# Prompt values in fp32, query copies and rope keys moved ahead, pages turned by sequence and fetched in halves, in a two-layer MLA and RG-LRU decoding step

## The reference, cut to what matters

```python
def mla_scores(q_lat, q_pe, ckv, kpe):
    s = jnp.einsum('bthc,blc->bhtl', q_lat, ckv, preferred_element_type=jnp.float32)
    s = s + jnp.einsum('bthr,blr->bhtl', q_pe, kpe, preferred_element_type=jnp.float32)
    return s * SM_SCALE
```

## Time and profile before

| | us |
|---|---|
| median of 3 runs | 1817.2 (1814.12 to 1818.85) |
| the profiled execution | 1814.61 |
| its span, first to last instruction | 1812.8 |
| last pair of the prompt attention, its 16 steps | 62.2 |
| decode attention, up to the first turn of probabilities | 64.0 |
| decode attention, from there to the last value product | 360.0 |

### The profile page before, as it was taken

The page is one execution under the profiler, slowest core; times in us unless marked ns, Lnnn a source line. Parts: engine busy times, 40 slices in busy tenths (PEclk is TensorE's granted clock), DMA queues, the critical chain, the costliest instruction groups (busy, mean ns, idle before and its releaser), DMA issues. The chain is left out here.

```text
span 1812.8 us, 26109 instructions
## 1 busy us (share of the span) xinstructions
PE 1433.7 (79%) x10731; PEld 1138.1 (63%) x10731; DVE 785.7 (43%) x1099; ACT 521.2 (29%) x741; POOL 152.1 (8%) x132
## 2 busy tenths in 40 slices
PE   4679998598988889717878878779969999750697
PEld 1279997377776777613444444447849999750485
DVE  0151010547373645626666656523236620349532
ACT  3321112134242433301111111223333232463332
POOL 0000000000000000020111111001220000025122
PEclk7769999699999989958889888889979999875799
DMA  9921110210010100092666655225321110100322
GB/s 328 341 59 36 46 35 25 60 30 1 23 29 23 29 23 0 0 357 46 238 242 236 244 233 233 117 89 167 120 69 47 46 46 12 47 0 0 131 96 78
DMA packets 98192, 180.39 MB, mean 100 GB/s; under 512 B 14245, under 2 KB 68395, under 8 KB 94026
## 3 DMA queue, kind: packets, MB, share of 16 engines
q1 hardware_dynamic: 88906, 95.50, 16.5%
q0 software_dynamic: 9216, 83.89, 11.7%
HBM read 162.10 MB, written 14.65 MB: 98 GB/s over the span
## 5 line engine op out<-in xcount | busy, mean ns | idle before, releaser
L80 PE MATMUL bank<-in_x_hi,in_w_hi 128*128 128x272 f32 x992 | 289.2, 291 | 19.2 <-DVE in_x_lo L413 19.2
L81 PE MATMUL bank<-in_x_lo,in_w_hi 128*128 128x272 f32 x992 | 289.1, 291 | 0.0
L82 PE MATMUL bank<-in_x_hi,in_w_lo 128*128 128x272 f32 x992 | 288.7, 291 | 0.0
L80 PEld LDWEIGHTS bank<-in_x_hi,in_w_hi 128*128 128x128 f32 x992 | 189.3, 191 | 19.4 <-issue 19.3
L82 PEld LDWEIGHTS bank<-in_x_hi,in_w_lo 128*128 128x128 f32 x992 | 189.0, 190 | 0.0
L81 PEld LDWEIGHTS bank<-in_x_lo,in_w_hi 128*128 128x128 f32 x992 | 188.9, 190 | 0.0
L1201 PE MATMUL bank<-u_T,q_rows 32*64 32x512 f32 x2560 | 156.2, 640 | 33.2 <-DMA q_rows<-qpe_blocks 33.2
L1096 DVE STREAM_TRANSPOSE u_T<-ckv_pages 128x1024 f32<-128x1024 f32 x128 | 147.4, 1209 | 69.1 <-DMA ckv_pages<-in_cache_ckv,page_parts 68.7
L403 DVE TENSOR_TENSOR in_w_lo<-in_w_raw,in_w_hi 128x1024 fp32r<-128x1024 f32 x31 | 38.0, 1225 | 239.4 <-ACT in_w_hi L355 239.3
L1201 PEld LDWEIGHTS bank<-u_T,q_rows 32*64 32x64 f32 x2560 | 55.8, 144 | 124.1 <-issue 87.0
L80 PE MATMUL bank<-out_w_hi,out_g_hi 128*128 128x512 f32 (+1 forms) x288 | 115.0, 399 | 13.0 <-DVE out_w_lo L1428 13.0
(11 more groups left out here) (259 smaller groups left out, 2534.8 us busy)
## 6 DMA issues: line engine op xcount, KB each, us to landing
u_T<-in_w_ada SPq DMA_DIRECT2D x12, 2048.0 KB, 14.5
in_w_raw<-in_r_w_in SPq DMA_DIRECT2D x16, 512.0 KB, 3.8
in_w_raw<-in_a_w_in SPq DMA_DIRECT2D x15, 512.0 KB, 4.0
x_tiles<-in_x_prompt SPq DMA_DIRECT2D x8, 512.0 KB, 9.6
g_mid<-u_T SPq DMA_DIRECT2D x4, 1024.0 KB, 4.0
out_w_raw<-in_a_w_o SPq DMA_DIRECT2D x8, 512.0 KB, 7.0
u_T<-g_mid SPq DMA_DIRECT2D x8, 512.0 KB, 5.9
out_x_in<-in_x_prompt SPq DMA_DIRECT2D x8, 512.0 KB
```

The costliest lines, as they stand in the source:

```text
L80: pe.matmul(out, w_hi, x_hi, start=start, stop=False)
L81: pe.matmul(out, w_hi, x_lo, start=False, stop=False)
L82: return pe.matmul(out, w_lo, x_hi, start=False, stop=stop)
```

## The change

- `values` of the prompt attention is one fp32 product for each key block instead of three fp32r ones. `v_all` and `p_T` are plain fp32 copies. The subtractions for `v_lo` and `pt_lo` are gone, and with them the waits for them; `turn` and `values` wait for ACT's copy (`pt_sb`).
- `q_rows` is allocated earlier. SP copies the queries of the first two sequence pairs inside `prompt_attention`, once the last head pair's queries are kept, and before the last spill. The part ends when they have landed.
- POOL fetches the rope keys of steps 0 and 1 there too, once three spills are done.
- A step's first chunk is now the rope keys, and the four latent chunks follow. DVE's order in step x is: last latent chunk of x, rope keys of x + 1, `maximum(x)`, three latent chunks of x + 1 for sequence 0, the same for sequence 1, `accumulate(x - 1)`. The rope keys of step 0 are turned before the new tokens' scores. `ckv_in` and `kt_set` are counted by sequence.
- The latents are fetched in halves, 8 KB for each partition (8 of its 16 rows), two gathers each. The first half of x + 3 waits for the second quad of `values(x)`, the second half for the fourth. The rope keys of x + 2 are fetched when those of x are turned. POOL's order is rope keys of x + 2, then latents of x + 3. DVE makes the indices of the halves (`halves`) in two operations.

```diff
-    v_hi, v_lo = sb("v_hi", [P, 8, 2 * P], F32R), sb("v_lo", [P, 8, 2 * P], F32R)
+    v_all = sb("v_all", [P, 8, 2 * P])
...
-    pt_hi, pt_lo = sb("pt_hi", [P, 8, 2 * P], F32R), sb("pt_lo", [P, 8, 2 * P], F32R)
+    p_T = sb("p_T", [P, 8, 2 * P])
...
+          spill((pr - 1) * 2, spilled)
+        sp.wait_ge(d_ev, NPAIR * D_N)
+        for pr in range(2):
+          copy_queries(sp, a, pr, qr_in)
...
-        spill(2 * NPAIR - 2)
-        sp.wait_ge(spilled, 16 * NPAIR)
+        spill(2 * NPAIR - 2, last_spilled)
+        sp.wait_ge(spilled, 16 * (NPAIR - 1))
+        sp.wait_ge(last_spilled, 16)
+        sp.wait_ge(qr_in, 16 * 32 * 2)
+        sp.wait_ge(kpe_first, 16 * 4)
+
+      @block.gpsimd
+      def _(pool):
+        pool.wait_ge(spilled, 16 * (NPAIR - 1))
+        for x in range(2):
+          load_rope_keys(pool, io, u_T, a, x, kpe_first)
       @block.scalar
...
-          act.activation(v_hi[:].rearrange("p (a b) n -> p a (b n)", a=4), region(1), ACT.Copy).then_inc(a_ev, 1)
+          act.activation(v_all[:].rearrange("p (a b) n -> p a (b n)", a=4), region(1), ACT.Copy).then_inc(a_ev, 1)
...
-          low(1, 10, v_lo[:].rearrange("p (a b) n -> p a (b n)", a=4), region(1),
-            v_hi[:].rearrange("p (a b) n -> p a (b n)", a=4))
...
-
-          def low_turned(s):
-            i, slot = s % 8, P * (s % 2)
...
-              dve.wait_ge(pt_hi_d, pr * GROUPS + (gi + 1))
-              dve.tensor_tensor(pt_lo[:, 4 * g:4 * g + n, slot:slot + P],
-                       bank[:, 4 + gi % 2, 0:P * n].rearrange("p (j q) -> p j q", q=P),
-                       pt_hi[:, 4 * g:4 * g + n, slot:slot + P].bitcast(F32), ALU.subtract
-                       ).then_inc(pt_lo_d, 1)
...
-            low_turned(s)
...
           project(0, lambda c: w_uk[:, c, 0:P], kv, VC, 256)
+          pe.wait_ge(a_ev, pr * A_N + 10)
+          project(1, lambda c: w_uk[:, c, P:2 * P], kv, VC, 256)
           pe.wait_ge(d_ev, pr * D_N + 12)
-          project(1, lambda c: w_uk[:, c, P:2 * P], kv, VC, 256)
-          pe.wait_ge(d_ev, pr * D_N + 13)
...
-                pe.wait_ge(pt_lo_d, pr * GROUPS + (gi - 1))
+                pe.wait_ge(pt_sb, pr * GROUPS + (gi - 1))
...
-            pe.wait_ge(pt_lo_d, pr * GROUPS + first_group(s + 1))
+            pe.wait_ge(pt_sb, pr * GROUPS + first_group(s + 1))
...
-              mm = split_matmul(pe, bank[:, 6 + bp % 2, q], v_hi[:, j, v], v_lo[:, j, v],
-                       pt_hi[:, j, q], pt_lo[:, j, q], j == 0, j == top)
+              mm = pe.matmul(bank[:, 6 + bp % 2, q], v_all[:, j, v], p_T[:, j, q], start=(j == 0), stop=(j == top))
...
-          pe.wait_ge(d_ev, pr * D_N + 16)
+          pe.wait_ge(d_ev, pr * D_N + 15)
...
-          pe.wait_ge(pt_lo_d, pr * GROUPS + GROUPS)
+          pe.wait_ge(pt_sb, pr * GROUPS + GROUPS)
           pe.wait_ge(o_out, pr * 8 + 8)
+
+
+def copy_queries(sp, a, pr, copied):
+
+  qr, half = a["qr"], H * NTOK
+  for r in range(4):
+    rows = slice(32 * r, 32 * r + 32)
+    for q in range(4):
+      sp.dma_start(qr[rows, pr % 2, q:q + 5:4, :],
+            a["qlat"][32 * q:32 * q + 32, :, 2 * pr:2 * pr + 2, :].rearrange("p c b q -> p c (b q)")).then_inc(copied, 16)
+    for s in range(2):
+      for e in range(2):
+        sp.dma_start(qr[rows, pr % 2, 8 + e, half * s:half * s + half],
+              a["qpe"][ROPE * s + 32 * e:ROPE * s + 32 * e + 32, pr, half * s:half * s + half]).then_inc(copied, 16)
+
+
+def load_rope_keys(pool, io, u_T, a, x, loaded):
+
+  pr, g = divmod(x, GROUPS)
+  for s in range(2):
+    at = 2 * GROUPS * pr + 2 * g + s
+    pool.indirect_dma_start(u_T[:, 8 + 2 * (x % 2) + s, 0:NP], None, io["cache_kpe"][0].rearrange("n (q j) c -> (n q) (j c)", q=PPP),
+                bass.IndirectOffsetOnAxis(a["parts"][:, at:at + 1], 0)).then_inc(loaded, 16)
...
+    ckv_in = [[sem(f"ckv_in{i}_{s}") for s in range(2)] for i in range(SLOTS)]
...
+    kt_set = [sem(f"d_kt_set{s}") for s in range(2)]
...
+    halves, halves_set = sb("half_parts", [P, 2, NB * GROUPS], I32), sem("halves_set")
...
-        queries(0)
-        queries(1)
...
-          queries(pr)
+          copy_queries(sp, a, pr, qr_in[pr % 2])
...
       @block.gpsimd
       def _(pool):
-        def load_kpe(x):
+        def load_ckv(x, half):
           pr, g = divmod(x, GROUPS)
           for s in range(2):
             at = 2 * GROUPS * pr + 2 * g + s
-            pool.indirect_dma_start(kpe_raw(x, s), None, io["cache_kpe"][0].rearrange("n (q j) c -> (n q) (j c)", q=PPP),
-                        bass.IndirectOffsetOnAxis(a["parts"][:, at:at + 1], 0)).then_inc(kpe_in[x % 2], 16)
-
-        def load_ckv(x):
-          pr, g = divmod(x, GROUPS)
+            rows = slice(J // 2 * half, J // 2 * half + J // 2)
+            pool.indirect_dma_start(ckv[:, x % SLOTS, s, rows, :].rearrange("p j c -> p (j c)"), None,
+                        io["cache_ckv"][0].rearrange("n (q h j) c -> (n q h) (j c)", q=PPP, h=2),
+                        bass.IndirectOffsetOnAxis(halves[:, half, at:at + 1], 0)
+                        ).then_inc(ckv_in[x % SLOTS][s], 16)
+
+        pool.wait_ge(halves_set, 2)
+        for x in range(SLOTS):
+          for half in range(2):
+            load_ckv(x, half)
+        for x in range(STEPS - 2):
           for s in range(2):
-            at = 2 * GROUPS * pr + 2 * g + s
-            pool.indirect_dma_start(ckv[:, x % SLOTS, s, :, :].rearrange("p j c -> p (j c)"), None,
-                        io["cache_ckv"][0].rearrange("n (q j) c -> (n q) (j c)", q=PPP),
-                        bass.IndirectOffsetOnAxis(a["parts"][:, at:at + 1], 0)).then_inc(ckv_in[x % SLOTS], 16)
-
-        for x in range(SLOTS):
-          load_ckv(x)
-          if x < 2:
-            load_kpe(x)
-        for x in range(2, STEPS):
-          pool.wait_ge(kt_set, 2 * (CPS * (x - 2) + CPS))
-          load_kpe(x)
-          if x + 1 < STEPS:
-            pool.wait_ge(v_quad, 4 * (x - 2) + 4)
-            load_ckv(x + 1)
+            pool.wait_ge(kt_set[s], CPS * x + 1)
+          load_rope_keys(pool, io, u_T, a, x + 2, kpe_in[x % 2])
+          if x + SLOTS < STEPS:
+            for half in range(2):
+              pool.wait_ge(v_quad, 4 * x + 2 * half + 2)
+              load_ckv(x + SLOTS, half)
       @block.scalar
...
       def _(dve):
-        def turn_keys(n):
+        def turn_keys(n, seqs=(0, 1)):
           x, cp = divmod(n, CPS)
-          if cp == 0:
-            dve.wait_ge(ckv_in[x % SLOTS], 32 * (x // SLOTS + 1))
-          if cp == CPS - 1:
-            dve.wait_ge(kpe_in[x % 2], 32 * (x // 2 + 1))
+          if cp == 0 and x >= 2:
+            dve.wait_ge(kpe_in[x % 2], 32 * (x // 2))
           if n >= RING:
             dve.wait_ge(kt_used, n - RING + 1)
-          for s in range(2):
-            src = (ckv[:, x % SLOTS, s, :, ROPE * cp:ROPE * cp + ROPE] if cp < CPS - 1
+          for s in seqs:
+            if cp == 1:
+              dve.wait_ge(ckv_in[x % SLOTS][s], 32 * (x // SLOTS + 1))
...
+        for half in range(2):
+          dve.tensor_scalar(halves[:, half, :], a["parts"][:], 2.0, float(half), ALU.mult, ALU.add).then_inc(halves_set, 1)
...
-        for n in range(RING):
+        for n in range(1, RING):
...
-        ahead = RING
         for x in range(STEPS):
-          for n in range(ahead, min(CPS * x + RING + CPS - 1, CPS * STEPS)):
-            turn_keys(n)
-          ahead = CPS * x + RING + CPS - 1
+          turn_keys(CPS * x + RING)
+          if x + 1 < STEPS:
+            turn_keys(CPS * (x + 1))
           maximum(x)
-          if ahead < CPS * STEPS:
-            turn_keys(ahead)
-            ahead += 1
+          if x + 1 < STEPS:
+            for s in range(2):
+              for cp in range(1, RING):
+                turn_keys(CPS * (x + 1) + cp, (s,))
...
-          if g == 0:
-            pe.wait_ge(qr_in[pr % 2], 32 * 16 * (pr // 2 + 1))
+          if g == 0 and pr >= 2:
+            pe.wait_ge(qr_in[pr % 2], 32 * 16)
           if x:
             pe.wait_ge(e_done, x)
           for cp in range(CPS):
             n = CPS * x + cp
-            pe.wait_ge(kt_set, 2 * n + 2)
+            for s in range(2):
+              pe.wait_ge(kt_set[s], n + 1)
             for hb in range(2):
-              cb = 2 * cp + hb
+              cb = 2 * ((cp - 1) % CPS) + hb
...
-                         start=(cb == 0), stop=(cb == 2 * CPS - 1), tile_position=(32 * r, HALF * s))
+                         start=(cp == 0 and hb == 0), stop=(cp == CPS - 1 and hb == 1), tile_position=(32 * r, HALF * s))
             mm.then_inc(kt_used, 1)
...
+      a["qr"] = own("q_rows", [P, 2, 10, P])
```

More of the change, by code:

```diff
@@ L678, in load, with spill @@
                                      ).then_inc(wkv_in, 16)
-                def spill(z):
+                def spill(z, spilled):
                     sp.dma_start(g_mid[ds(z, 2)].rearrange("c p t -> p c t"), u_T[:, ds(z + Z_M, 2), 0:NP]).then_inc(spilled, 16)
@@ L730, in keep_turned @@
```

(24 more changed lines are left out.)

18 lines of the change are left out of this document (8 added, 10 removed).

## The result

The changed kernel takes 1709.2 us (median of 4 runs, 1707.67 to 1710.06), against 1815.7 for the kernel before beside it (4 runs). The ratio is 0.9412, 95% interval 0.9393 to 0.9431: 106 us less. I had forecast 1670 with a range that ended at 1708, so nearly 40 us of the forecast gain did not come, and the time lies 1.2 us outside the range. The profiled execution took 1710.06 us, its span 1708.3.

What follows compares the result with a forecast made beforehand. TensorE has the most work in both loops yet waits, for VectorE, query copies and pages. Prompt values 54, decode start 31 and steps 62 make 147 us off 1814.6, so 1667.6, stated as 1670; range 1642 to 1708.

Steps and rivals of the forecast that it cites:

- The fp32 product: Prompt values: one fp32 product takes 0.22 us against 0.36 for three fp32r, saving 0.14 a block, 22 us in all.
- The sign that the prediction names for being wrong: Prompt values: fp32 products at 0.4 us or more would show the forecast wrong.
- Rival F: Prompt values: fp32 products take 0.44 us a block, as at half clock; 1705 us, or 1711 by four passes; chance 1%.
- The waits of the prompt part: Prompt attention: waits for VectorE's subtractions shrink by 7.0 us a pair, 28 in all, and `v_lo` waits by 3.4.
- Start of decode: Decode start: early query copies and rope keys bring the first turn from 839.46 to 808.5, 31 us; bounds 24 and 36.
- The cover: Last prompt pair's step loop: the 64 query copies take 41 us and fit under it with 5 us to spare, costing nothing.
- Rival D: End of prompt: the query copies don't fit under the loop, 118 us for 64; 1742 us; chance 5%.
- Steps: Sixteen decode steps: alternate waits for rope keys, 38.2 us per two steps, 360.0 to 298, saving 62; bounds 281 and 315.
- A: Decode steps: alternate short waits for rope keys as in the main forecast; 1670 us, range 1650 to 1692; chance 55%.
- B: Decode steps: rope keys land before the scores end and TensorE is the bound, 17 us less; 1653 us; chance 15%.
- C: Decode steps: the halved fetches, or one wait per step, are dearer; 1694 us; chance 20%.
- E: Decode page fetches: 8 KB rows slow the gather; 1765 us at 26 us a step, 1820 at 30; chance 3%.

Runs made afterwards that it cites:

- run 4: Changed kernel with three fp32r products of the same high halves per key block for the prompt values instead of one fp32 product, no low halves: 1700.8 us.
- run 8: Changed kernel with the 64 query copies of the first two sequence pairs issued at the start of the decode part again: 1735.7 us.
- Run 5: Changed kernel with POOL fetching the rope keys of step x+3 ahead of both halves of that step's pages: 1663.0 us.
- run 6: Changed kernel with pages fetched whole, two fetches of 16 KB rows a step, after the last quad of values(x): 1730.2 us.
- run 7: Changed kernel with both halves of each page fetched late, after the last quad of values(x): 1734.0 us.

## Why the prediction was wrong

The mechanisms were those forecast. Two terms of the sum had the wrong size, the price of an fp32 product, which had the wrong sign too, and the landing of the rope keys; and one was put at nothing but in the first decode step: what TensorE's products take behind a wait, at a lower clock.

**The fp32 product.** The step that failed: "32 fp32 products of the same 128x256 shape take 7.07, so 0.22 each. Per block 0.14 is saved." The row counts records, and an fp32 product has two. 7.07 us are 16 products of 0.44, against 0.36 for three fp32r products. By this the edit costs 0.08 a block of 256 columns, some 12 us, instead of giving 22; run 4 measured 1.9 us a pair, 7.6 in all, since narrow blocks cost no more. The sign that the prediction names for being wrong, fp32 products at 0.4 us or more, came. A look at the code, where that loop issues 8 x 2 products, would have told it. The same row bears out the four passes of the Trainium skill (FP8 and Floating Point Precision, TensorE Precision Notes, on true FP32): four of the 0.12 us that the earlier trace rows give for an fp32r product are 0.48, and 0.44 was measured. My sentence that the trace doesn't agree was wrong. Rival F had the right pitch, 0.44, and gave it 1%, for a reason (a half clock) that wasn't the cause: the clock of that loop was 1.00. That its 1705 and its 1711 lie nearest to the measured 1709.2 is luck: the product cost 7.6 us, not 13 or 19, and the largest part of the miss lay in the decode steps.

**The waits of the prompt part.** Forecast 28 us, and 3.4 for `v_lo`, 31.4 together. The waits bear it out nearly to the digit: 38.9 - 10.7 = 28.2, and 3.4. Run 4 has the same by another way, 7.9 us less idle time a pair, 32 over four. But the stage won more than its waits: 11.1 us a pair is 44 over four. The other 13 are TensorE's busy time, 3.2 us a pair less for the same products. The prediction has no term for it, and the granted clock of the pairs, 0.95 to 0.98 before and 0.98 to 1.00 in run 4, can account for most of it (the estimate under run 4); how much comes from restarting behind fewer waits no run tells apart. 44 less 7.6 is 37, as measured. The forecast of 54 was one term wrong by some 30 us, hidden in part by this one of 13.

**Start of decode.** 31 forecast, 32.6 measured. The cover held. SP's last copies and the last spill after them:

```profile
726.38 2.49 SPq L937 DMA_DIRECT2D q_rows<-qpe_blocks  x4
737.97 0.41 SPq L681 DMA_DIRECT2D g_mid<-u_T  x1
```

The copies are issued 9 us before the spill (5 forecast). Rival D is out; run 8 gives its mechanism the price of 26 us.

**Steps.** Forecast 298 us, measured 325.5: this is the largest miss, and it lies outside the bounds of 281 to 315. The pattern was right: a wait of TensorE in every second step, for rope keys and not for pages. In the changed kernel the steps with a wait took 22.5 us on average and those without 19.65 (seven of each, the first step left out), 42.2 together, not 38.2. The 4.0 a pair have two causes.
- "So the rope keys land at V - 3.2 + 16.1 = V + 12.9." They were turned at V + 15.2 on average over the steps that waited, 18.4 after the first page fetch and not 16.1. That is 2.2 us a pair. Most of it is a reading of the kernel before. VectorE waits for both rope fetches. The 16.1 adds the offset of the first (2.5 us behind the first page fetch) to the median landing of both. The second is issued 3.7 behind, and in the kernel before it landed 16.8 to 18.6 after the first page fetch, 17.4 on average over the five steps that fetch both. The pair of the earlier trace rows, whose pages were asked for at 1095.15:

```profile
1098.88 0.94 POOL L1010 DMA_INDIRECT u_T<-in_cache_kpe,page_parts  x1 [0.30 <-issue]
DMA to landing us min/median/max: 13.2/13.2/13.2
```

So 1.3 of the 2.2 us stood in the trace already. Of the rest, whole pages have 17.75 from the first page fetch to the turn, halves late 18.25 and the changed kernel 18.35. Cutting the pages into four fetches adds some 0.5 us. The second half's wait for the last quad, which moves the rope keys' issue to 5.95 and 7.2 behind the first fetch, adds 0.1. The 0.35 between 17.4 and 17.75 is not traced.
- "After one such wait the next step has 2.4 us more." The next step also has TensorE at a lower clock. I priced that once, at the first step ("2 for slow products after the wait"), and not at the seven waits behind it: 19.65 - 17.9 = 1.75 us each. Run 5 takes the waits away and every step is 17.9.

With these two a pair is 38.2 + 2.2 + 1.75 = 42.2, and the sum is 21 + 7 x 42.2 + 9.5 = 326. My other bound, "a wait in every step, 315", left the clock out as well.

**The rivals.** A came true in form and missed in size. B's outcome, TensorE as the bound, needs an earlier issue of the rope keys; with it the steps take 280 us (281 forecast). C's halves cost some 0.5 us a step (runs 6 and 7), which the times don't tell from nothing; its 1694 was too low. What C weighed from the Trainium skill (DMA: Bandwidth & Descriptors, Measured), 15.4 us for a step's 5.24 MB, is nearer to the traces than the 13.2 us that B took from the 396 GB/s of the earlier trace rows, which is the middle of a transfer. From a step's first packet to its last it is, in the kernel before, with whole pages and in the changed kernel (DMA share and GB/s stand last):

```profile
1096.70:1111.60 14.90, 14.90 (x216) 7.94 (x202) 4.37 (x4) 1.09 (x2) 2.51 (x3) 1.00 0.89 354
794.70:809.30 14.60, 14.60 (x214) 7.73 (x200) 2.54 (x3) 1.09 (x2) 2.48 (x3) 1.00 0.91 361
793.60:809.80 16.20, 16.20 (x228) 8.55 (x226) 5.95 (x7) 2.17 (x4) 4.33 (x5) 1.00 0.84 325
```

But the 2 MB fetches of the first two rows are below 396 as well, so it isn't the size of a fetch alone. E did not happen; its sum, 1670 + 97, is 1767 and not 1765, and the 1820 beside it should be 1822.

## What to carry to other kernels

- Before a duration is divided by the count of a row, compare the count with what the code issues. A row counts records, and an instruction can leave two.
- When a wait goes away, price what TensorE does behind it too: here each wait of 3.6 to 5.9 us left 1.75 us of slow products in the next step, and without the seven of them, 32 us, the steps were 46 us shorter. In the prompt part of run 4, 32 us of idle time went and the stage won 44.
- Where an engine waits for several fetches, take the time from the one that lands last, and its own issue: the median over all of them was 1.3 us too early here.
- When a fetch is moved ahead, follow the smallest and last fetch behind it on the same queue. Here two fetches of 0.5 MB of rope keys behind 4 MB of pages set the pace, and one change of order on POOL gave 46 us, more than the halved fetches.

## What the runs showed of the hardware

- An fp32 product of 128 x 128 by 256 columns takes 0.44 us at a clock of 1.00 and leaves two records; one in fp32r takes 0.12, three of them 0.36 to 0.37. With 128 columns one in fp32 takes 0.27 to 0.28, and one in fp32r 0.11 (in the kernel before 731.39, 731.50, 731.61), hardly less than with 256. A turn through the identity by 128 columns, fp32 too, has one record (288 of them for the 288 that the code issues).
- Four fetches of 1 MB in rows of 8 KB, asked for at once, take nearly the time of two of 2 MB in rows of 16 KB: the rope keys behind them were turned 0.5 us later (run 7 against run 6), and the whole times differ by less than their intervals. The packets grow from 9216 to 13824 for the same 83.89 MB.
- The 64 query copies cost the prompt loop above them nothing. The last pair's loop with them, in the table of stages, has TensorE busy 50.51 of 55.00 us at a clock of 1.00; without them, in run 8, it is

```profile
681.90:736.90 55.00, 50.52 (x302) 43.24 (x300) 28.84 (x76) 24.48 (x57) 0.00 (x0) 1.00 0.00 0
```
